# A convolution and sparse-attention layer on one core: head outputs put together on GpSimd instead of VectorE

## What is computed

```python
def block(i):
    score = jnp.einsum('bqh,bqhs->bqs', wi_b, jax.nn.relu(dots))
    score = jnp.where(causal[None], score, -jnp.inf)
    _, sel = lax.top_k(score, topk)
    logits = jnp.einsum('bqhd,bqkhd->bqhk', q_b, k[sel]) * att_scale
    p = jax.nn.softmax(jnp.where(valid, logits, -jnp.inf), axis=-1)
    return jnp.einsum('bqhk,bqkhd->bqhd', p, v[sel])
...
y_conv = group_rmsnorm(y_conv, gn_conv, CONV_GROUPS) * jax.nn.silu(cz)
y_attn = group_rmsnorm(y_attn, gn_attn, N_HEADS) * jax.nn.silu(az)
y = jnp.concatenate([y_conv, y_attn], axis=-1) @ w_out
h = x + gate[:, None, :] * y
return rmsnorm(h, norm_f)
```

## Time and profile before

| | |
|---|---|
| Time, median of 3 runs | 687.44 us (686.63 to 687.79) |
| The profiled execution, its own time | 687.08 us |
| Its span in the trace | 685.3 us |
| PE busy | 653.4 us, 95% of the span |
| DVE busy | 452.0 us, 66% |
| ACT busy | 376.0 us, 55% |
| POOL busy | 240.9 us, 35% |
| Granted TensorE clock, mean over the span | 0.997 |

### The profile page before, as it was taken

The page is one execution under the profiler, slowest core; times in us unless marked ns, Lnnn a source line. Parts: engine busy times, 40 slices in busy tenths (PEclk is TensorE's granted clock), DMA queues, the critical chain, the costliest instruction groups (busy, mean ns, idle before and its releaser), DMA issues.

```text
span 685.3 us, 8984 instructions
## 1 busy us (share of the span) xinstructions
PE 653.4 (95%) x3203; PEld 547.1 (80%) x3203; DVE 452.0 (66%) x750; ACT 376.0 (55%) x547; POOL 240.9 (35%) x133
## 2 busy tenths in 40 slices
PE   0999999999999999999999999999999999999996
PEld 0888987878888888888888888788788887778884
DVE  5884646767889999996038751003899998577625
ACT  6866445655562132444552453444899999874202
POOL 1001234343334152657545856540037635000000
PEclk9999999999999999999999999999999999999998
DMA  8960596443333111111010361134885451222431
GB/s 321 380 229 1 144 170 149 136 155 94 93 92 119 35 50 44 55 38 60 32 63 31 124 215 61 32 89 96 276 193 117 125 124 42 84 92 100 147 123 61
DMA packets 27911, 78.64 MB, mean 115 GB/s; under 512 B 3986, under 2 KB 8410, under 8 KB 27868
## 3 DMA queue, kind: packets, MB, share of 16 engines
q1 hardware_dynamic: 27524, 77.03, 37.5%
q10 hardware_dynamic: 344, 1.05, 0.6%
HBM read 61.25 MB, written 13.41 MB: 109 GB/s over the span
## 4 chain that ended last, share of the span: by engine, by line
PE 82%; DVE 6%; ACT 4%; issue 3%; DMA 2%; POOL 2%; SPq 1%; DVEq 0%; ACTq 0%; POOLq 0%
PE ps L810 17%; PE ps L812 17%; PE ps L811 17%; PE ps L1025 4%; PE ps L1026 4%; PE ps L1027 4%; PE ps L847 3%; PE ps L880 2%; PE ps L881 2%; PE ps L899 2%; PE ps L900 2%; PE ps L968 2%; PE ps L967 2%; PE ps L700 1%; DVE acc L1485 1%
## 5 line engine op out<-in xcount | busy, mean ns | idle before, releaser
L810 PE MATMUL ps<-hH,wH 128*128 128x512 f32 (+1 forms) x544 | 211.7, 389 | 0.1
L812 PE MATMUL ps<-hH,wL 128*128 128x512 f32 (+1 forms) x544 | 210.1, 386 | 0.0
L811 PE MATMUL ps<-hL,wH 128*128 128x512 f32 (+1 forms) x544 | 210.1, 386 | 0.0
L1864 POOL TENSOR_TENSOR wL<-raw,wH 128x1024 fp32r<-128x1024 f32 x35 | 87.7, 2507 | 183.2 <-ACT wH L1083 175.0
L812 PEld LDWEIGHTS ps<-hH,wL 128*128 128x128 f32 x544 | 102.1, 188 | 20.4
L810 PEld LDWEIGHTS ps<-hH,wH 128*128 128x128 f32 x544 | 102.1, 188 | 20.3 <-issue 1.7
L811 PEld LDWEIGHTS ps<-hL,wH 128*128 128x128 f32 x544 | 102.2, 188 | 18.4
L1285 ACT ACTIVATE relu<-ps,wabs 128x384 f32<-128x384 f32 (+5 forms) x48 | 40.1, 849 | 39.5 <-PE ps L900 15.9
L1588 DVE SCALAR_TENSOR_TENSOR score<-relu,wsgn,score 128x384 f32<-128x384 f32 (+5 forms) x42 | 49.7, 1184 | 13.7 <-ACT relu L1285 10.2
L1609 DVE TENSOR_SCALAR_CACHE_REDUCE above<-score,srch 128x384 bf16<-128x384 f32 (+5 forms) x60 | 56.8, 946 | 2.1
L1704 DVE TENSOR_TENSOR phL<-ps,phH 128x512 fp32r<-128x512 f32 (+1 forms) x80 | 49.1, 632 | 10.9 <-ACT phH L1241 10.0
(11 more groups left out here) (240 smaller groups left out, 1170.9 us busy)
## 6 DMA issues: line engine op xcount, KB each, us to landing
raw<-in_w_units SPq DMA_DIRECT2D x36, 512.0 KB, 3.5
ks<-qk_halves SPq DMA_DIRECT2D x32, 256.0 KB, 5.8
xin<-in_x SPq DMA_DIRECT2D x8, 512.0 KB, 7.4
wa<-in_w_ada SPq DMA_DIRECT2D x8, 512.0 KB, 12.1
wa<-in_w_ada SPq DMA_DIRECT2D x16, 256.0 KB, 7.7
gw<-in_w_ada SPq DMA_DIRECT2D x8, 512.0 KB, 4.2
qs<-qk_halves SPq DMA_DIRECT2D x16, 256.0 KB, 4.0
wo<-in_w_out SPq DMA_DIRECT2D x8, 512.0 KB, 7.6
```

What stands on the lines that cost most here:

```text
L810: pe.matmul(out, wH[slot(n)][:, kt, :], hH[:, kt, cols], start=(kt == 0), stop=False)
L811: pe.matmul(out, wH[slot(n)][:, kt, :], hL[:, kt, cols], start=False, stop=False)
L812: mm = pe.matmul(out, wL[slot(n)][:, kt, :], hH[:, kt, cols], start=False, stop=(kt == KT - 1))
L1864: g.tensor_tensor(wL[slot(n)][:], raw[slot(n)][:], wH[slot(n)][:].bitcast(F32), ALU.subtract).then_inc(s_wL, 1)
```

## The change

1. **Head outputs.** For the first 14 of the 16 halves (`SHIFTED`, heads 0 to 6) ScalarE copies the whole bank, 128 rows by 512 columns, out of PSUM: to `ya` for an even head, to a new buffer `obuf` for an odd one. SyncE then shifts the 64 rows of the other half by a DMA to `tmp` (`shift_out`), and GpSimd adds the two in SBUF (`join`). TensorE's waits for the bank are for the copy (`out_read`), no longer for the sum. The last head's two halves stay as before.
2. **Squares.** Of each of the first three pairs only the first half's square is still split; the second half's is summed by a plain fp32 matmul.
3. **Loads.** A head's queries and keys come as two parts of 512 columns, three DMAs of 128 partitions each. The first four blocks of the output weights are loaded after head 2's loads, blocks 4 and 5 one round later. The store of the denominators' row (`keep_row`) stands ahead of the second part of the loads, and its reading back after it.
4. **Tables.** The places of logits, maxima, exponentials, denominators and sums are others.

```diff
-LOGITS_AT = (1, 3, 10, 13, 14, 15, 16, 18)
-MAX_AT = (1, 2, 9, 14, 14, 15, 15, 18)
-EXP_AT = (9, 13, 13, 16, 16, 17, 19, 21)
+LOGITS_AT = (2, 5, 5, 11, 16, 16, 18, 20)
+MAX_AT = (0, 4, 6, 10, 15, 16, 17, 20)
+EXP_AT = (6, 9, 15, 18, 18, 19, 21, 24)
...
-TMP_AT, OUT_AT = 5, 5
+TMP_AT, OUT_AT = 4, 5
+SHIFTED = 2 * (NH - 1)
...
-DSQ_AT = {HEAD * (2 * t + 1) + (5 if t < NT - 1 else 5): t for t in range(NT)}
-DENS_AT = {HEAD * (2 * t + 1) + (11 if t < NT - 1 else 7): t for t in range(NT)}
-KEEP_AT = {HEAD * (2 * t + 1) + (13 if t < NT - 1 else 9): t for t in range(NT)}
-SUMS_AT = {HEAD * (2 * t + 2) + 5 + 8 * half: (t, half) for t in range(NT - 1) for half in range(2)}
+DSQ_AT = {HEAD * (2 * t + 1) + (4 if t < NT - 1 else 5): t for t in range(NT)}
+DENS_AT = {HEAD * (2 * t + 1) + (9 if t < NT - 1 else 7): t for t in range(NT)}
+KEEP_AT = {HEAD * (2 * t + 1) + (14 if t < NT - 1 else 9): t for t in range(NT)}
+SUMS_AT = {HEAD * (2 * t + 2) + 7 + 8 * half: (t, half) for t in range(NT - 1) for half in range(2)}
...
-KEEP_SUMS_AT = {HEAD * (2 * t + 2) + 5 + 8 * half: (t, half) for t in range(NT - 1) for half in range(2)}
+KEEP_SUMS_AT = {HEAD * (2 * t + 2) + 7 + 9 * half: (t, half) for t in range(NT - 1) for half in range(2)}
...
+        obuf = at("obuf", [P, HALF], F32, 12)
...
+        def out_read(engine, g):
+            if g < SHIFTED:
+                engine.wait_ge(s_tmp, g + 1)
+            else:
+                engine.wait_ge(s_o, g - SHIFTED + 1)
...
+            def load_head(h, part):
+                if h == 2 and part == 0:
+                    sp.wait_ge(s_unit, NU)
+                if h >= 2 and part == 0:
+                    sp.wait_ge(s_lg, NB * (h - 1))
+                if h:
+                    sp.wait_ge(s_stack[part], 48 * h)
+                cols = slice(HALF * part, HALF * part + HALF)
+                sp.dma_start(qs[h % 2][:, cols].bitcast(F32), dqk[0, :, h, :, cols]).then_inc(s_stack[part], 16)
+                for i, dst in enumerate((ks1, ks2)):
+                    sp.dma_start(dst[h % 2][:, cols].bitcast(F32),
+                                 dqk[1, i:i + 1, h, :, cols].broadcast_to([2, HD, HALF])).then_inc(s_stack[part], 16)
+            def shift_out(g):
+                sp.wait_ge(s_tmp, g + 1)
+                if g:
+                    sp.wait_ge(s_join, g)
+                r, d = rows(g // 2), rows(g // 2 + 1)
+                sp.dma_start(tmp[r, :], kept_out(g)[d, :]).then_inc(s_shift, 16)
...
             for h in range(NH):
+                if h:
+                    shift_out(2 * h - 1)
+                if h + 2 < NH:
+                    load_head(h + 2, 0)
+                if h == 0:
+                    load_head(2, 1)
+                if h < NH - 1:
+                    shift_out(2 * h)
+                if h % 2 and h < NH - 1:
+                    keep_row(h // 2)
+                if h == 0:
+                    for ct in range(4):
+                        sp.dma_start(wo[:, ct, :], a["w_out"][P * ct:P * ct + P, :]).then_inc(s_wo, 16)
+                elif h + 2 < NH:
+                    load_head(h + 2, 1)
...
                 if bank == 6:
-                    pe.wait_ge(s_o, 2 * h + 1 if at_step > 5 else 2 * h - 1)
+                    out_read(pe, 2 * h if at_step > 5 else 2 * h - 2)
...
                 act.wait_ge(s_pv, last_chunk(g) + 1)
-                if g >= 1:
-                    act.wait_ge(s_o, g)
-                A(tmp[r, :], ps[d, 6 + sb, :], ACT.Copy).then_inc(s_tmp, 1)
+                if g < SHIFTED:
+                    if h % 2 and g > 2:
+                        act.wait_ge(s_join, g if sb else g - 2)
+                    A(kept_out(g), ps[:, 6 + sb, :], ACT.Copy).then_inc(s_tmp, 1)
...
+            def join(g_):
...
+                pool.wait_ge(s_shift, 16 * (g_ + 1))
...
+                g.tensor_tensor(ya[r, h // 2, HALF * sb:HALF * sb + HALF], kept_out(g_)[r, :], tmp[r, :],
+                                ALU.add).then_inc(s_join, 1)
```

More of the change, by code:

```diff
@@ L394, in build @@
         s_wo = sem("s_wo"); s_woH = sem("s_woH"); s_woL = sem("s_woL"); s_woLd = sem("s_woLd")
-        s_stack = [sem(f"s_stack{i}") for i in range(2)]
+        s_stack = [sem(f"s_stack{part}") for part in range(2)]
         s_vh = sem("s_vh"); s_vv = sem("s_vv")
@@ L471, in wo_high, with squared @@
             return hH[:, ct, :] if ct < 4 else woB[ct // 2 - 2][:, ct % 2, :]
+        def squared(t, half):
+            return 4 * t + half + (3 if t < NT - 1 else 1)
         def sums_bank(t, half):
@@ new lines, in shift_out @@
+            def shift_out(g):
[4 more added lines that the diff above has]
+                sp.dma_start(tmp[r, :], kept_out(g)[d, :]).then_inc(s_shift, 16)
+            for h in range(2):
+                for part in range(2):
+                    load_head(h, part)
+            for h in range(NH):
+                if h:
[13 more added lines that the diff above has]
+                    load_head(h + 2, 1)
+                if h == 2:
+                    sp.wait_ge(s_wo, 16 * 4)
+                    for ct in range(4, KT - 2):
@@ L986, in group_sums @@
                 else:
-                    pe.wait_ge(s_o, 2 * NH)
-                if t == NT - 1:
+                    out_read(pe, 2 * NH - 1)
+                if t == NT - 1 or half:
                     mm = pe.matmul(ps[:, sums_bank(t, half), :], pairs[:], ysq[:], start=True, stop=True)
@@ L1013, in out_step @@
                     elif half == 0:
-                        pe.wait_ge(s_o, 2 * NH - 1)
+                        out_read(pe, 2 * NH - 2)
                     else:
@@ L1781, in _ @@
                         row_max(u)
-                    if x in OUTS:
+                    if x in OUTS and OUTS[x] >= SHIFTED:
                         head_out(OUTS[x])
@@ L1927, in _ @@
                     mm.then_inc(s_vv, 1)
-            def pair_square(t, half):
-                pool.wait_ge(s_o, 4 * t + half + 3)
+            def join(g_):
+                h, sb = g_ // 2, g_ % 2
+                r = rows(h)
+                pool.wait_ge(s_shift, 16 * (g_ + 1))
+                if g_ % 4 == 3:
+                    pool.wait_ge(s_ygP, g_ // 2)
+                elif g_ % 4 == 2:
+                    pool.wait_ge(s_join, g_)
+                elif g_ % 4 == 0 and g_:
+                    pool.wait_ge(s_ygP, g_ // 2)
+                elif g_ == 1:
+                    pool.wait_ge(s_join, 1)
+                elif g_ % 4 == 1:
+                    pool.wait_ge(s_woL, g_ // 4 + 1)
+                g.tensor_tensor(ya[r, h // 2, HALF * sb:HALF * sb + HALF], kept_out(g_)[r, :], tmp[r, :],
+                                ALU.add).then_inc(s_join, 1)
+            def pair_square(t, half):
+                if t < NT - 1:
+                    pool.wait_ge(s_join, 4 * t + half + 3)
+                else:
+                    pool.wait_ge(s_join, 4 * t + half + 1)
+                    pool.wait_ge(s_o, half + 1)
                 if t or half:
@@ L1958, in pair_add @@
                 pool.wait_ge(s_sums, 2 * t + half + 1)
+                if half == 0:
+                    pool.wait_ge(s_join, 4 * t + 5)
                 pool.wait_ge(s_din, 32 * (t + 1))
@@ L1963, in _ @@
             for t in range(NT - 1):
+                if t == 0:
+                    join(0)
+                join(4 * t + 1)
+                join(4 * t + 2)
                 pair_square(t, 0)
                 pair_gate(t, 0)
+                join(4 * t + 3)
                 pair_square(t, 1)
                 pair_gate(t, 1)
+                join(4 * t + 4)
                 pair_add(t, 0)
@@ L1972, in _ @@
                     out_split(1)
+            join(SHIFTED - 1)
             pair_square(NT - 1, 0)
```

59 lines of the change are left out of this document (31 added, 28 removed).

## The result

| | before | changed |
|---|---|---|
| Median of 5 runs each | 687.15 us (686.02 to 687.79) | 852.1 us (851.5 to 852.87) |
| Ratio | | 1.2407, interval 1.2393 to 1.2421 |
| Span of the profiled execution | 685.3 us | 851.0 us |
| PE busy | 653.4 us | 687.5 us |
| Granted TensorE clock, mean | 0.997 | 0.915 |

The change makes the kernel 24% slower, 165 us. The forecast was 685.2 us and the range ended at 688.8, so it was wrong by far. No rival came near it either.

A forecast was written before the change was run, and what follows sets the result against it. TensorE was taken as the bound, busy 106.0 of 110 us in the attention stage. Terms of -3.8 + 0.9 + 0.7 = -2.2 us took the median of 687.44 us to a forecast of 685.2 us, range 682.7 to 688.8.

The forecast's parts named there:

- Loads: Key and query loads in the attention stage: six DMAs a head as before, as many bytes, so no cost.
- Stalls won: TensorE's nine stalls behind VectorE's head outputs or the squares they feed: 3.8 of 4.2 us won.
- late logits: Chain from each head's last logits (i = 7) loses its slack: 0.1 us each, 0.7 us added.
- fp32 sums: Second halves' squares summed on TensorE by plain fp32, 0.86 us against 0.57, three times: 0.9 us added.
- Shift: DMA of 128 KB for each of 14 head outputs: 2.2 us to landing, with 5.8 as the far end.
- join: GpSimd's addition for each of 14 head outputs: 1.3 us each.
- copies no dearer: ScalarE's copies out of PSUM, 128 rows in place of 64: 0.598 us against 0.593, counted as nothing.
- no contention with VectorE: GpSimd's additions of two SBUF inputs beside VectorE's PSUM-reading instructions in the stage: no slowdown counted.
- Rival C: Shift landing takes over 2.9 us, so the second half's sum stalls; at 3.9 us, 688.2 us; chance 0.06.
- The tables: New places in the attention stage: most effects counted elsewhere; the chain after the last logits adds 0.7 us.
- A: ScalarE is the attention stage's next bound, so only half of the 3.8 us comes: 687.1 us; chance 0.27.
- B: Chain of the last logits (i = 7) costs a ScalarE copy each head, 3.5 us: 688.0 to 689.9; chance 0.10.

## Why the prediction was wrong

**The step that failed** is *Loads*: "Six DMAs a head as before, as many bytes" and "Nothing". I counted DMAs and bytes, and never asked over how many DMA engines each is spread. What was put at nothing is the 165 us: with this form alone changed back the kernel takes 686.86 us in place of 852.1, and with this form alone put into the kernel before it takes 844.59. The diff shows it: `dqk[0, :, h, :, cols]` and `broadcast_to([2, HD, HALF])` have an outer dimension of 2, where the loads before have 64 rows outermost. In the trace of before, loads in flight show a DMA share of 0.98 at 232 GB/s:

```profile
456.00:466.00 10.00, 10.00 (x46) 8.29 (x45) 0.00 (x0) 1.09 (x2) 2.39 (x1) 1.00 0.98 232
```

In the changed kernel it is 0.13 at 51 GB/s. With 12.6 MB to move and a stage of 122 us, 51 GB/s had to become the bound: 247 us for the loads alone. That product, 125 us more than the stage, would have shown a loss of this order, though not its size: the lower clock and the queue come on top.

The Trainium skill has this (DMA: Bandwidth & Descriptors, the section on why a DMA increments its semaphore by 16, on how many engines): a DMA goes to the largest number of engines up to 16 that divides the slowest dimension, not counting those of size 1, of both sides. The rules for kernel authors on the same page of the Trainium skill add that a leading broadcast of c copies, with c under 16, confines it to at most c. By that rule it is 2 engines here; the trace agrees, with 0.13 of 16, and with 0.26 for an outer dimension of 4. I had read that page for its fixed cost and not for this, and it should have been a rival.

Two consequences make up the rest. TensorE, idle for loads, is granted half its clock in stretches, which adds 34 us to its busy time; how much of this the waits for loads would have taken in its place was not separated. And the queue: an issue that waits 5.0 us holds up shifts and the denominators' row, and so the 36.7 us of waits for squares. A shift also took 13.0 us from the start of its issue to its landing, in the median:

```profile
DMA to landing us min/median/max: 2.2/13.0/16.3
```

The shortest are the last two, issued when no load was left. That the others wait for the two engines full of loads shows in the packets of the first: its issue ends at 542.45, from 543.0 to 543.85 us 14 end marks of 4 bytes (one for each engine that is done) come in together with the packets of most of its rows, and the join still waits until 553.85 us. Till 552.7 us packets of 2 KB, the size of the loads' and of the shift's, go on at 16 to 25 in a microsecond, where two engines alone moved 25.

**The other terms** can be read with the loads mended. I added up TensorE's starts from the first turn to the last values as in the prediction: usual distances by kind, and what exceeds them by over 0.1 us. The rest of each row, 5.9 to 6.8 us, is excess of less than that. The second column depends on what is taken as usual: with the median distance of each kind, before and the third row differ by 0.9 us and not by 1.5. The third column moves by up to 0.6 us.

| | stage, us | usual distances | stalls |
|---|---|---|---|
| before | 121.6 | 108.5 | 6.7 |
| before, new tables only | 125.9 | 108.3 | 11.4 |
| changed, six DMAs a part | 121.8 | 110.0 | 5.0 |
| changed, queries in one DMA | 119.65 | 110.0 | 3.0 |
| the same, second square split | 125.7 | 108.8 | 10.4 |
| changed, whole loads at one place | 126.7 | 110.0 | 10.8 |

- *Stalls won, -3.8 us, and late logits, +0.7*: together -3.1. Measured -1.7 with six DMAs a part, since one shift behind other DMAs gives a new stall of 1.33 us, and -3.7 where nothing holds the shift up. The mechanism was right, and the size too where the queue is clear. The late logits alone, +0.7, were 0.1 us in each of seven heads in the sum; TensorE waits 0.8 us in one head and nowhere else, so that the term has the right size is luck.
- *fp32 sums, +0.9 us*: 1.2. A sum takes 0.96 us to the next turn where TensorE had stood still before it, and the two split products 0.57 there. Where nothing stalls it is 0.86 (543.58 to 544.45 with the queries in one DMA) against 0.47 (537.81 to 538.27 before). Each pair differs by 0.39, three times is 1.2, and taking the split back gives the same 1.2 (110.0 to 108.8). My 0.86 from the earlier trace rows was right, but I took it against the 0.57 of a row behind a stall. The other 0.3 us of the table's 1.5 is within what the choice of usual distances does.
- *Shift 2.2 us, join 1.3 us, copies no dearer, no contention with VectorE*: right, 2.3 to 2.7 in the median, 1.28, 0.593, and VectorE's operations kept their durations (its 80 low parts are 50.56 us before and 50.61 after). Rival C's price for a late shift was right as well, 1 us at a landing of 3.9 us against the 1.33 measured at 3.85; it came once and not three times.
- *The tables*: without the rest of the change they cost 3.3 us (690.43 less 687.18 in medians, 4.3 in the stage). That is not their price in the changed kernel: the waits are for head outputs on VectorE and their squares, which the change takes away. They and the head outputs are one change: on these tables, the rest of it with mended loads brings some 3.2 us (+3.3 us against its kernel before becomes +0.04), while all together bring nothing over before.

So with the loads mended the sum of -2.2 us came out at +0.2 in the stage: the stalls gave 1.7 us in place of 3.1, the fp32 sums cost 0.3 more than forecast, and some 0.7 us, the 0.3 above and 0.4 in excesses of less than 0.1, isn't placed.

The stages and the medians agree to some 1 to 2 us only, since the profiled executions begin the stage at times that differ by up to 2.2 us, and lie up to 1.0 us beside the median of their kernel; so differences under 1 us in this table prove nothing by themselves.

**Rivals.** A (half of the gain, -0.3 us) is what the mended kernel shows in size, but ScalarE is at most a part of the reason: TensorE waits 0.8 us for one exponential in it, and 1.3 us for a late shift. B shows at its place in the last head alone, 0.8 us and not 3.5. C's mechanism is in two kernels, with whole loads at one place and in one stall of the mended one. None of them touches the 165 us.

What stays open is why the gain of 1.95 us in the stage with the queries in one DMA shows as 0.12% of the median and no more. In the profiled execution 1.66 us of it were lost before the stage began, and why it began later isn't known: with the same layout in DRAM another kernel began at 479.13 us.

## What to carry to other kernels

Before a DMA is counted by bytes, read its access pattern's outer dimension: 2 there means 2 of 16 engines and about 50 GB/s, however wide the DMA is. Here it was the source that had 2, 4 or 16 outermost, while the destination was a tile of 128 partitions; the other way round was not run. In a profile this shows as waits for DMAs together with a DMA share of a fixed small fraction, 0.13 or 0.26, and as issues in the queue that take microseconds each. Two DMAs of 64 rows are then far better than one of two by 64. And where a change gives a helper engine a chain through a queue (copy, shift, join), the loads in that queue have to be cut in parts, or they eat the gain: whole loads at one place cost 5.5 us here (692.38 against 686.86).

## What the runs showed of the hardware that was not expected

- An outer dimension of 2, 4 and 16 gave DMA shares of 0.13, 0.26 and 0.98, and 51 to 53, 106 and 241 GB/s while loads were in flight; the time of the kernel was 844.59, 738.56 and 688.48 us.
- SyncE's issue of a 256 KB DMA, 0.58 us when the queue is free, takes 5.0 us behind such DMAs, and what is behind it waits with it though only two packets are in flight.
- A shift of 128 KB behind such DMAs took 13.0 us in the median to land, where it takes 2.2 with nothing before it: most of its rows were moved within 1.4 us of its issue's end, and the rest waited.
- With every compute engine idle for 6 us the granted clock was 0.54, and 0.50 in a stretch in which TensorE was busy for under half.
